# First feed-forward as a block product with seven multiplications instead of eight, on aligned tiles, with the up unit's last product ahead of the gate's in every pair

## The reference

```python
x = x + merged @ w_out[i]
h = rms_norm(x, norm_ffn[i])
x = x + (jax.nn.silu(h @ w_ffn_gate[i]) * (h @ w_ffn_up[i])) @ w_ffn_down[i]
gate = jax.nn.sigmoid(rms_norm(x, norm_ple[i]) @ w_ple_gate[i])
x = x + gate * (p[i] @ w_ple_proj[i])
...
c_act = jax.nn.silu(c)
mod = c_act @ w_ada[l] + b_ada[l]
```

## Time and profile before

| | |
|---|---|
| median of 3 executions | 2864.58 us (2863.87 to 2868.34) |
| the profiled execution, its own time | 2865.05 us |
| its span in the trace | 2863.2 us |
| PE busy | 97% of the span, 12600 matmuls |
| DVE, ACT, POOL busy | 46%, 32%, 28% |
| granted TensorE clock, mean | 0.992 |

### The profile page before, as it was taken

The page is one execution under the profiler, slowest core; times in us unless marked ns, Lnnn a source line. Parts: engine busy times, 40 slices in busy tenths (PEclk is TensorE's granted clock), DMA queues, the critical chain, the costliest instruction groups (busy, mean ns, idle before and its releaser), DMA issues.

```text
span 2863.2 us, 30939 instructions
## 1 busy us (share of the span) xinstructions
PE 2772.2 (97%) x12600; PEld 2225.0 (78%) x12600; DVE 1320.2 (46%) x1464; ACT 911.7 (32%) x1453; POOL 811.7 (28%) x436
## 2 busy tenths in 40 slices
PE   8999999999999999999999999998999999999997
PEld 6666778887788888888877677877757888888885
DVE  6777842231434333433353646436274343434446
ACT  6666521121311111111154333355353221222223
POOL 2444522223222222222244221134432222222225
PEclk9999999999999999999999999999999999999998
DMA  3000011121123222221112102122321111111113
GB/s 116 23 23 23 11 56 48 44 98 64 67 89 111 102 89 89 90 95 45 67 45 99 68 31 44 35 74 63 125 81 45 58 45 52 44 48 49 49 47 132
DMA packets 65133, 184.98 MB, mean 65 GB/s; under 512 B 6616, under 2 KB 20184, under 8 KB 64864
## 3 DMA queue, kind: packets, MB, share of 16 engines
q1 hardware_dynamic: 64992, 183.01, 18.8%
HBM read 167.71 MB, written 15.27 MB: 64 GB/s over the span
## 4 chain that ended last, share of the span: by engine, by line
PE 85%; DVE 6%; ACT 3%; issue 3%; POOL 2%; DMA 1%; SPq 0%; POOLq 0%; DVEq 0%; ACTq 0%
PE psum_mem L559 65%; PE psum_mem L955 2%; PE psum_mem L960 2%; PE psum_mem L957 2%; PE psum_mem L619 2%; PE psum_mem L603 1%; PE psum_mem L654 1%; PE psum_mem L709 1%; PE psum_mem L657 1%; PE psum_mem L655 1%; POOL w_lo L3092 1%; PE psum_mem L1032 1%; PE psum_mem L997 1%; PE psum_mem L1297 1%; PE psum_mem L706 1%
## 5 line engine op out<-in xcount | busy, mean ns | idle before, releaser
L3092 POOL TENSOR_TENSOR w_lo<-w_raw,w_hi 128x1024 fp32r<-128x1024 f32 (+1 forms) x233 | 548.0, 2352 | 1730.4 <-ACT w_hi L1322 1730.3
L559 PE MATMUL psum_mem<-h_hi,w_hi 128*128 128x512 f32 x2096 | 656.0, 394 | 19.4 <-ACT h_hi L1355 8.8
L559 PE MATMUL psum_mem<-h_hi,w_lo 128*128 128x512 f32 x2096 | 651.1, 392 | 7.7 <-POOL w_lo L3092 7.7
L559 PE MATMUL psum_mem<-h_lo,w_hi 128*128 128x512 f32 x2096 | 650.8, 392 | 3.6 <-DVE h_lo L2914 2.7
L559 PEld LDWEIGHTS psum_mem<-h_hi,w_hi 128*128 128x128 f32 x2096 | 395.2, 189 | 108.4 <-ACT h_hi L1355 8.8
L559 PEld LDWEIGHTS psum_mem<-h_hi,w_lo 128*128 128x128 f32 x2096 | 395.4, 189 | 93.8 <-POOL w_lo L3092 11.4
L559 PEld LDWEIGHTS psum_mem<-h_lo,w_hi 128*128 128x128 f32 x2096 | 395.9, 189 | 89.7 <-DVE h_lo L2914 4.2
L1322 ACT CAST w_hi<-w_raw 128x1024 fp32r<-128x1024 f32 (+1 forms) x233 | 234.1, 1005 | 605.2 <-PE psum_mem L559 486.7
L2150 DVE TENSOR_TENSOR tmp_mem<-psum_mem,norm_row 128x1024 f32<-128x1024 f32 x44 | 53.9, 1224 | 280.5 <-PE psum_mem L559 280.4
L2475 DVE TENSOR_TENSOR x_block<-x_block,psum_mem 128x1024 f32<-128x1024 f32 x88 | 107.3, 1219 | 66.1 <-PE psum_mem L559 63.5
L3142 POOL TENSOR_TENSOR beta<-beta,left 128x128 f32<-128x128 f32 (+2 forms) x96 | 87.8, 917 | 141.0 <-DVE left L2266 140.1
(11 more groups left out here) (382 smaller groups left out, 4131.0 us busy)
## 6 DMA issues: line engine op xcount, KB each, us to landing
ada_raw<-in_w_ada SPq DMA_DIRECT2D x48, 512.0 KB, 4.5
w_raw<-in_w_up_b SPq DMA_DIRECT2D x44, 512.0 KB, 3.3
w_raw<-in_w_in_a SPq DMA_DIRECT2D x32, 512.0 KB, 3.3
w_raw<-in_w_ffn_gate SPq DMA_DIRECT2D x22, 512.0 KB, 3.6
w_raw<-in_w_ffn_up SPq DMA_DIRECT2D x22, 512.0 KB, 3.4
w_raw<-in_w_ffn_down SPq DMA_DIRECT2D x22, 512.0 KB, 4.5
w_raw<-in_w_down_b SPq DMA_DIRECT2D x22, 512.0 KB, 3.3
w_raw<-in_w_in_b_ml SPq DMA_DIRECT2D x16, 512.0 KB, 3.3
```

Of the source, the lines that this page charges most:

```text
L559: made = e.matmul(pairs.half(use, half), wt, x[:, half_of(half)], start=at == 0 and part == 0, stop=at == len(rhs) - 1 and part == 2, skip ...
L3092: e.tensor_tensor(w_lo[:, i, 0:width], w_raw[:, i, 0:width], w_hi[:, i, 0:width].bitcast(F32), ALU.subtract).then_inc(*S.of("w_lo", c))
```

## The change

**The block product.** Up tile i and gate tile i are now made together as a 2 x 2 block product: rows are (up, gate), the inner dimension is cut into two halves of four blocks (KH = 4), and the tokens into two halves of 512. Seven products of 12 matmuls replace eight: `UP_LOW`, `SUM_2`, `DIFF_3`, `SUM_1`, `UP_HIGH`, `DIFF_4`, `GATE_HIGH`. Three of them need sums of weights (`weight_low_sum`, three DVE instructions per pair, and `weight_high_sum`, one), and activations come in seven forms (`form_hi`, `form_lo`), built once while w_out ends. The high and low weights now lie in four slots of 128 x 512; product j uses slot j % 4, so UP_HIGH, GATE_HIGH and DIFF_4 reuse the slots of UP_LOW, SUM_2 and DIFF_3. Each pair uses three PSUM banks, and accumulates UP_HIGH on UP_LOW's bank, SUM_1 and then DIFF_4 on SUM_2's, and GATE_HIGH on DIFF_3's. Between these, partial values leave the banks: ACT copies "low", "two" and "four" to `parts`, DVE adds in place (`b_sum`) and reads the gate's halves (`gate_read`).

**The order.** Pairs and down steps are listed in `FF_ORDER`: pairs 0, 1, 2, down 0, pairs 3, 4, down 1, and so on to down 8, pairs 19, 20, 21, down 9, down 10. The hidden tiles now have one buffer, and two extra tiles for the last pairs. In every pair DIFF_4 comes before GATE_HIGH on PE.

**The modulation** moves from the feed-forward to the gates and branches. It is cut into 96 steps of 128 x 512 with three raw buffers (one is a piece of `merged`), and 4, 5, 3 and 2 steps follow the four phases of each m. Its 12 PE sums have four columns each.

**SP** now issues the first three w_out units ahead of the eight loads of x1; before, it was two.

The diff, cut to what the prediction speaks of (PE's `product` and its order, the modulation sums, then a part of ACT's pair loop, and last SP's waits):

```diff
+def first_ffn_order():
+    order = []
+    for i in range(KF):
+        order.append(("pair", i))
+        if i % 2 == 0 and 2 <= i < HID_LAST:
+            order.append(("down", i // 2 - 1))
+    return order + [("down", N_GROUPS - 2), ("down", N_GROUPS - 1)]
...
+UP_LOW, SUM_2, DIFF_3, SUM_1, UP_HIGH, GATE_HIGH, DIFF_4 = range(7)
...
+        ADA_AFTER = (4, 5, 3, 2)
...
+            def product(i, j, blocks=range(KH)):
+                for event in {UP_LOW: (("up", (i - 2, 0)),), SUM_2: (("up", (i - 2, 1)),), DIFF_3: (("gate", (i - 2, 0)),),
+                              UP_HIGH: (("part", (i, "low")),), SUM_1: (("part", (i, "two")),),
+                              GATE_HIGH: (("gate", (i, 1)),), DIFF_4: (("part", (i, "four")),)}[j]:
+                    if i >= 2 or j > DIFF_3:
+                        w.wait_ge(*event)
...
+                elif at == 0:
+                    product(0, SUM_2, range(KH - 1))
+                    product(0, UP_LOW)
+                    product(0, DIFF_3, range(KH - 1))
+                    product(0, SUM_2, (KH - 1,))
+                    product(0, DIFF_3, (KH - 1,))
+                    product(0, UP_HIGH)
+                    product(0, SUM_1)
+                    sum_first()
+                    product(0, DIFF_4)
+                    product(0, GATE_HIGH)
+                else:
+                    for j in (UP_LOW, SUM_2, DIFF_3, SUM_1, UP_HIGH, DIFF_4, GATE_HIGH):
+                        product(at, j)
...
             for m in range(KD):
                 if m == 0:
                     map_group(0)
                     map_group(1)
+                for q in mod_ended(m - 1, (2, 3)):
+                    modulation(q)
                 one("w_ga", ("ga", m), h_rhs("a"), (("g_a", m),))
+                for q in mod_ended(m, (0,)):
+                    modulation(q)
                 one("w_gb", ("gb", m), h_rhs("a"), (("g_b", m),))
+                for q in mod_ended(m, (1,)):
+                    modulation(q)
...
+                w.wait_ge("b_sum", i)
+                if i > 0:
+                    w.wait_ge("gate", (i - 1, 0))
+                part(i, "two", 1)
...
+                w.wait_ge("full", ("gu", i, SUM_1))
+                part(i, "four", 0)
...
+                gate_silu(i, 1)
+                if down_behind(i) is not None:
+                    for slot in range(4):
+                        fill_down(down_behind(i), slot)
+                        if slot == 1:
+                            gate_silu(i, 0)
+                elif i < KF - 1:
+                    if i > 0:
+                        fill_pair(i + 1, UP_LOW)
+                    fill_pair(i + 1, SUM_2)
+                    gate_silu(i, 0)
+                    fill_pair(i + 1, DIFF_3)
+                    fill_pair(i + 1, SUM_1)
...
+                    if n >= N_RAW:
+                        w.wait_ge("ada", divmod(n - N_RAW, KD))
+                    else:
+                        w.wait_ge("u_centred", 3)
```

More of the change, by code:

```diff
@@ L781, in tensor, with modulation @@
             rhs_b = [(yb_hi[:, k, :], yb_lo[:, k, :], (("yb_hi", k), ("yb_lo", k))) for k in range(4)]
+            def modulation(q):
+                use = ("mod", q)
+                for event in pairs.take(use, (("mod", q),)):
+                    w.wait_ge(*event)
+                w.wait_ge("ada", (q, KD - 1))
+                for j in range(KH):
+                    made = e.matmul(pairs.whole(use)[:, j:j + 1], ada_sum[q % 2][:, block_of(j)], const("ones", 1),
+                                    start=True, stop=True, skip_group_check=True)
+                made.then_inc(*S.of("full", use))
             for m in range(KD):
@@ L811, in hidden @@
                         for i in range(FFN_GROUP)]
-            def modulation(part):
-                use = ("mod", part)
-                for event in pairs.take(use, (("mod", part),)):
-                    w.wait_ge(*event)
-                w.wait_ge("ada", (part, KD - 1))
-                for j in range(KD):
-                    made = e.matmul(pairs.whole(use)[:, j:j + 1], ada_sum[part % 2][:, block_of(j)], const("ones", 1),
-                                    start=True, stop=True, skip_group_check=True)
-                made.then_inc(*S.of("full", use))
@@ new lines, in late_scaled, with form_sums @@
+            def late_scaled(k):
+                if k > 0:
+                    w.wait_ge("form", (SUM_1, k - 1))
+                w.wait_ge("x1", ("out", k))
+                e.activation(parts[:, 0, :], x1[:, k, half_of(1)], ACT.Copy, bias=0.0,
+                             scale=vec("norm_ffn", k)).then_inc(*S.of("part", ("late", k)))
+                form_high(UP_LOW, k, x1[:, k, half_of(0)], vec("norm_ffn", k))
+            def form_sums(k):
+                w.wait_ge("form", (DIFF_3, k))
+                form_high(DIFF_3, k, parts[:, 1, :])
+                w.wait_ge("form", (SUM_2, k))
+                form_high(SUM_2, k, form_raw[:, 7, :])
@@ new lines, in scalar, with part, hidden_high @@
+            fill_pair(0, SUM_1)
+            form_sums(KH - 1)
+            form_high(UP_HIGH, KH - 1, x1[:, KD - 1, half_of(0)], vec("norm_ffn", KD - 1))
+            def part(i, name, at):
+                e.copy(parts[:, at, :], gu_bank(i, {"low": UP_LOW, "two": SUM_2, "four": SUM_1}[name])).then_inc(
+                    *S.of("part", (i, name)))
+            def hidden_high(i):
+                w.wait_ge("up", (i, 0))
+                w.wait_ge("up", (i, 1))
+                if i >= HID_LAST:
+                    w.wait_ge("full", ("gu", KF - 1, DIFF_4))
+                elif i >= 2:
+                    w.wait_ge("full", ("w_down", i // 2 - 1, KD - 1))
+                e.copy(hidden_first(hid_hi_a, hid_hi_last, i), tmp[:, i % 2, :]).then_inc(*S.of("hid_hi", ("a", i)))
@@ new lines, in vector, with b_sum @@
+                if m == 6:
+                    form_low(UP_LOW, KH - 1, x1[:, KH - 1, half_of(0)], vec("norm_ffn", KH - 1))
+                    for k in range(2):
+                        form_low(SUM_1, k, form_raw[:, KH + k, :])
+            form_one(KH - 1)
+            for k in range(KH):
+                form_low(UP_HIGH, k, x1[:, KH + k, half_of(0)], vec("norm_ffn", KH + k))
+            def b_sum(i):
+                w.wait_ge("part", (i, "low"))
+                w.wait_ge("full", ("gu", i, SUM_2))
+                out = gu_bank(i, SUM_2)
+                e.tensor_tensor(out, out, parts[:, 0, :], ALU.add).then_inc(*S.of("b_sum", i))
@@ new lines, in gate_read, with gate_norm @@
+            def gate_read(i, half):
+                s = tmp[:, i % 2, half_of(half)]
+                w.wait_ge("part", (i, "four" if half else "two"))
+                w.wait_ge("full", ("gu", i, DIFF_3 if half else GATE_HIGH))
+                e.tensor_tensor(s, parts[:, 1 - half, :], gu_bank(i, DIFF_3), ALU.add).then_inc(*S.of("gate", (i, half)))
+            def gate_norm(i, half, name):
+                s = tmp[:, i % 2, half_of(half)]
+                w.own("gate")
+                e.tensor_tensor(s, s, norm_row[:, half_of(half)], ALU.mult).then_inc(*S.of(name, (i, half)))
@@ new lines, in sync @@
+            raw_emptied(ff_end - ff_first)
+            taken[0], done[0] = ff_end, ff_end
+            c = ff_end
+            for n in range(2):
+                if n:
+                    raw_emptied(ff_end - ff_first + 1)
+                e.dma_start(w_raw[:, n, 0:unit_width[c + n]], units[c + n][1]).then_inc(*S.of(f"in_w{n}", c + n, 16))
+                if n == 0:
+                    w.wait_ge("full", ("gu", KF - 1, DIFF_4))
+                    for k in range(2):
+                        e.dma_start(p_raw[:, k, :], io["p"][k]).then_inc(*S.of(f"in_p{k}", 0, 16))
```

725 lines of the change are left out of this document (511 added, 214 removed).

## The result

The changed kernel took 2835.51 us (median of 4 runs, 2834.71 to 2836.27), the kernel before 2864.22 us beside it (4 runs, 2863.38 to 2868.34). The ratio is 0.9897, 95% interval 0.988 to 0.9914: 29 us less, where 15 had been forecast (2850). The direction was right, the measured time lies inside the range of 2824 to 2868, and the size is wrong by nearly a factor of two. The likeliest case spanned 2838 to 2862 and does not hold the time.

What follows compares the result with a forecast made beforehand. PE, busy 97% of the span, was taken as the bound, so only fewer or cheaper matmuls help. Terms -59.8 + 10.0 + 1 - 3.6 + 12 + 19 + 6 = -15.4 gave 2850 us, range 2824 to 2868.

Steps and rivals of the forecast that it cites:

- likeliest case: Whole kernel: mostly as the terms say, with DVE and POOL taking turns; 2838 to 2862 us, chance 0.52.
- term f: Seams of the steady feed-forward: PE waits for the gate's chain at eleven direct seams and nine down steps; +19 us.
- two branches: At the seams: POOL first, 1.1 and 1.3 us each, 24 in all; DVE first, 0.4 and 0.6, 10 in all.
- Taking turns: DVE and POOL instructions with two SBUF operands hold each other up; 2850 us with turns, near 2828 without.
- b: Modulation at m = 0: PE waits 7.6 us for the first sum's load chain, 0.4 for weights, 2 of clock; +10.0 us.
- c: Modulation sums: twelve stops of four columns replace six of eight, the same matmuls but twelve refills; +1 us.
- d: w_out: third unit loaded ahead of x1 removes the 0.80 us cast wait, its idle time and clock loss; -3.6 us.
- e: Feed-forward's head: DVE's forms, taking turns with POOL, delay pairs 0 and 1; +12 us (-2 to +18).
- g: Down 9: two low parts ahead of DVE's first addition, 4.9 us of wait and 1.1 of clock; +6 us (3 to 8).
- The collisions bite less: Rival, seams and head: DVE first, queues slip past one another; f 9, e 3, g 3.5; 2828 us, chance 0.27.
- The gates stage short of DVE at every m: Rival, gates stage: sums wait 1 us at seven of the m, +10 with the clock; 2860 us, chance 0.11.
- the next up stripe late: Rival, direct seams: up weights landing after about 4.5 us delay 11 seams; at 6.5 us +22, 2872 us, chance 0.10.

Runs made afterwards that it cites:

- pool_first3: The changed kernel with 256 columns of gate_read done a second time ahead of gate_norm in every pair from 1 on; 2855.91 us.
- swap: The changed kernel with GATE_HIGH's product ahead of DIFF_4's in every pair from 1 on; 2821.61 us, ratio to before 0.9849.
- w_out_ahead: The kernel before with only the third w_out unit loaded ahead of x1; 2859.43 us beside 2862.78, ratio 0.9991.
- head_order: On swap with m = 0's modulation behind the pool maps (2810.48 us): SUM_1's low forms of k = 0 and 1 moved behind b_sum; 2810.74 us.
- tail: On swap: tile 20's high and low parts made in pair 21, and three pairs of PSUM banks for down 10; 2820.29 us.
- h20: On swap with m = 0's modulation behind the pool maps (2810.48 us): only tile 20's parts made in pair 21; 2809.03 us, ratio to before 0.981.

## Why the direction was right and the size wrong

**The step that failed is in term f**: "The requests are 0.04 us apart; I take two in three for POOL: +19." The two branches had been worked out as 24 and 10 us, and the second one happened, at 10.1 us lost: DVE was first at every seam, and gate_norm's first half took 0.69 us and not the 1.8 that the prediction gave as a sign. At the direct seam DVE saw the end of the gate's product 0.06 us before ACT did (847.66 and 847.72), whose cast releases POOL; at the down step both started at 806.22. The forecast had DVE behind ACT, 0.27 and 0.25, from two separate rows of the kernel before with other instructions. And from ACT's start to POOL's it took 0.76 us, 0.05 more than in the forecast. Two starts that differ by 0.02 us cannot carry a decision worth 14 us. The sum should have been made with the two branches kept apart, 2841 with f = 10 and 2855 with f = 24, and the likeliest case should have spanned both.

The branch that did not happen was priced well in its waits: pool_first3 shows 1.11 and 1.23 us where the forecast had 1.1 and 1.3. The stage from the first down step to down 9 lost 26.7 us there, for 24. The branch that did happen comes out at 10 by luck: its waits were half of the forecast, 0.19 and 0.35 us for 0.4 and 0.6, and each cost PE 0.3 us more than its bracket shows (last section), for which the forecast had nothing.

**Taking turns** is right. In the head, DVE's and POOL's rows alternate from 732.93 on, each at 1.6 to 1.8 us instead of 0.7 and 1.3:

```profile
732.93 1.61 POOL L3602 TENSOR_TENSOR w_lo<-w_sums,w_hi 128x512 fp32r<-128x512 f32 x1 [2.75 <-ACT w_hi L1722]
...
733.31 1.77 DVE L2750 TENSOR_TENSOR form_lo<-form_raw,form_hi 128x512 fp32r<-128x512 f32 x1
```

The Trainium skill (SBUF — State Buffer, "Who interferes with whom") says that the second of the two to issue blocks fully; the trace agrees at both seams above, with the loser changed as the order was. What the rule cannot say is who is second.

**b** (+10.0, measured +11.4 by rows; 9.6 us came back when it was undone on top of swap, where the wait was 7.92 us) is right in place, releaser and size: 8.36 us of wait for 7.6, then the next five rows of two matmuls took 4.36 us instead of 2.27. The wait of 0.4 us for ba(0)'s weights did not occur. **c** (+1, measured +0.2) was a little too dear: each sum takes 0.81 us and 0.13 behind it, and each of the six before took 1.70 and 0.14. **d** (-3.6, measured -4.2) is right, and w_out_ahead shows it by itself.

**e** (+12, measured +8.3): the addition of x1(7) began 7.8 us after w_out's end (740.11 less 732.34), forecast 9.3, and pair 0 and 1 have waits of 10.4 us, forecast 15.1. The turns and DVE's queue were as described, but DVE was through them 1.5 us earlier, and no clock was lost (1.00 in both windows, forecast 2.5 us). The stage lost 15.6 us all the same, 5 more than its waits; eleven restarts at some 0.3 us (last section), which the forecast left out, are the larger part of that. head_order shows that the stage is bound by DVE's work as such. **g** (+6, measured +9.0): the wait before m = 2 of down 9 was 3.52 us, forecast 4.9, but the thirteen starts behind it took 2.6 us more than at full clock, forecast 1.1. These two misses cancel. What is over are two waits in down 10 that the forecast lacked, 0.33 and 1.41 us. tail shows that PE waits there for banks that DVE's last additions free; that turns with POOL make these late is read from the durations of the low parts, not tried. By h20 only 1.1 us of the stage comes back easily.

**The rivals.** "The collisions bite less" (2828, chance 0.27) comes nearest, 7.5 us off, for its f of 9; its e of 3 and its g of 3.5 were too low. The gates stage short of DVE at every m, and the next up stripe late, did not occur: no wait for a modulation sum stands behind m = 0, and none for weights at a direct seam from the third pair on.

## What to carry to other kernels

When two engines ask for the same resource a few hundredths of a microsecond apart, work out both orders and forecast the pair of results; only a trace of the new program tells which happens. In a pipeline of products, put last the one whose consumer chain is shortest: here one line moved 14 us, about half as much as the whole change had brought, and it also made the contention harmless without removing it. Before moving small work beside a stage, ask where its first result is needed, not only whether the stage has room: seven modulation steps behind the maps cost nothing, eight in front of them cost 11 us.
